# Expert stage of a one-core MoE decoder layer: f32r-split weight products against plain f32 products, experts taken in pairs

## The reference

```python
def hier_moe(h, w_group, b_group, w_expert, b_expert, w_gate, w_up, w_down):
    ...                                   # top-1 group of 4, top-2 of its 8 experts
    gates = jnp.sum(jax.nn.one_hot(e_idx, N_EXPERTS) * wts[..., None], axis=1)
    def expert(acc, prm):
        wg, wu, wd, gt = prm
        hid = jax.nn.silu(h @ wg) * (h @ wu)
        return acc + gt[:, None] * (hid @ wd), None
    out, _ = lax.scan(expert, jnp.zeros_like(h), (w_gate, w_up, w_down, gates.T))
```

## Time and profile before

| | us |
|---|---|
| median of 3 runs | 792.78 |
| lowest, highest | 792.27, 794.53 |
| profiled execution: span | 794.2 |
| TensorE (PE) busy | 728.8 |
| VectorE (DVE) busy | 636.6 |
| ScalarE (ACT) busy | 526.4 |
| GpSimd (POOL) busy | 307.2 |
| HBM read | 248.30 MB, 314 GB/s over the span |

### The profile page before, as it was taken

The page is one execution under the profiler, slowest core; times in us unless marked ns, Lnnn a source line. Parts: engine busy times, 40 slices in busy tenths (PEclk is TensorE's granted clock), DMA queues, the critical chain, the costliest instruction groups (busy, mean ns, idle before and its releaser), DMA issues.

```text
span 794.2 us, 12672 instructions
## 1 busy us (share of the span) xinstructions
PE 728.8 (92%) x4733; PEld 570.3 (72%) x4734; DVE 636.6 (80%) x538; ACT 526.4 (66%) x544; POOL 307.2 (39%) x214
## 2 busy tenths in 40 slices
PE   3669999989679999999999999999999999999980
PEld 1248577544457888888888888888888888888860
DVE  3363294635648999999999999999999999999973
ACT  2020133455527887888888888878888888888761
POOL 7300000040053456654456644566544566544000
PEclk9979999999659999999999999999999999999996
DMA  8999987710528899999999999999999999999501
GB/s 337 357 405 379 367 313 275 292 69 0 212 76 309 319 383 378 372 367 370 383 379 364 377 371 372 381 381 369 372 373 381 365 383 369 371 375 372 202 0 61
DMA packets 102004, 249.78 MB, mean 315 GB/s; under 512 B 8134, under 2 KB 8146, under 8 KB 98898
## 3 DMA queue, kind: packets, MB, share of 16 engines
q1 hardware_dynamic: 96448, 244.33, 82.9%
q10 hardware_dynamic: 5092, 3.46, 1.4%
q0 software_dynamic: 432, 1.59, 0.6%
HBM read 248.30 MB, written 1.07 MB: 314 GB/s over the span
## 4 chain that ended last, share of the span: by engine, by line
PE 84%; DVE 5%; DMA 4%; POOL 2%; ACT 2%; issue 2%; ACTq 0%; DVEq 0%; POOLq 0%
PE PS L1250 45%; PE PS L1238 8%; PE PS L1218 7%; PE PS L1209 6%; PE PS L1042 5%; PE PS L1160 3%; PE PS L1036 3%; POOL line L373 2%; DMA toe<-line_dram 2%; PE PS L1228 1%; DMA tabT<-in_rel_bias_dram 1%; PE PS L1017 1%; DVE MOD L698 1%; DVE S L774 1%; DVE S L754 1%
## 5 line engine op out<-in xcount | busy, mean ns | idle before, releaser
L918 DVE TENSOR_TENSOR WL<-W,WH 128x2048 fp32r<-128x2048 f32 x187 | 419.8, 2295 | 7.1 <-ACT WH L619 7.1
L619 ACT CAST WH<-W 128x2048 fp32r<-128x2048 f32 x187 | 349.9, 1903 | 48.6 <-PE PS L1250 48.6
L416 POOL TENSOR_SCALAR OG<-slot_no,cur 128x128 f32<-128x128 f32 x64 | 161.7, 2531 | 0.0
L1250 PE MATMUL PS<-WH,XT 128*128 128x512 f32 x512 | 140.2, 396 | 0.6 <-DVE XT L928 0.6
L1250 PE MATMUL PS<-WL,XT 128*128 128x512 f32 x508 | 140.0, 397 | 0.0
L403 POOL COPY cur<-PG 128x4 f32 (+1 forms) x33 | 8.3, 251 | 274.8 <-PE PS L1228 227.3
L1250 PEld LDWEIGHTS PS<-WH,XT 128*128 128x128 f32 x512 | 97.0, 190 | 23.8 <-DVE XT L928 0.6
L1250 PEld LDWEIGHTS PS<-WL,XT 128*128 128x128 f32 x508 | 96.0, 189 | 22.4
L413 POOL TENSOR_SCALAR OH<-slot_no,cur 128x128 bf16<-128x128 f32 x64 | 106.5, 1674 | 0.0
L1250 PE MATMUL PS<-WH,HT 128*128 128x512 f32 x256 | 70.5, 398 | 1.5 <-issue 1.5
L698 DVE SCALAR_TENSOR_TENSOR MOD<-W,cS,MOD 128x2048 f32<-128x2048 f32 x20 | 46.9, 2347 | 30.1 <-DMA W<-in_w_ada_dram 29.8
(11 more groups left out here) (184 smaller groups left out, 762.3 us busy)
## 6 DMA issues: line engine op xcount, KB each, us to landing
W<-in_w_gate_dram SPq DMA_DIRECT2D x64, 1024.0 KB, 8.0
W<-in_w_down_dram SPq DMA_DIRECT2D x64, 1024.0 KB, 6.2
W<-in_w_up_dram SPq DMA_DIRECT2D x63, 1024.0 KB, 9.9
W<-in_w_ada_dram SPq DMA_DIRECT2D x24, 1024.0 KB, 8.1
W<-in_w_in_dram SPq DMA_DIRECT2D x12, 1024.0 KB, 13.2
W<-in_w_out_dram SPq DMA_DIRECT2D x4, 1024.0 KB, 11.6
toe<-line_dram POOLq DMA_DIRECT2D x1, 1536.0 KB, 14.5
X<-in_x_dram ACTq DMA_DIRECT2D x1, 1024.0 KB, 12.4
```

What stands on the lines that cost most here:

```text
L416: nc.gpsimd.tensor_scalar(OG[:, buf, t, :], slot_no[:], cur[:, buf, 0, t:t + 1], cur[:, buf, 1, t:t + 1], ALU.is_equal, ALU.mult).then_inc ...
L619: nc.scalar.copy(WH[:, (UPE * odd + u) % SPLITS, :], source).then_inc(hi_ready, 1)
L918: nc.vector.tensor_tensor(low, source, WH[:, (UPE * odd + u) % SPLITS, :].bitcast(f32), ALU.subtract).then_inc(lo_ready, 1)
L1250: last = nc.tensor.matmul(PS[:, bank, :], lhsT, w[:, q * 512:(q + 1) * 512], start=begin, stop=end)
```

## The change

The expert stage is rewritten. The weights are no longer split: TensorE multiplies the f32 units as they arrive in W, with f32 token blocks and f32 hidden blocks as 64-column stationary operands. WH, WL, H3, GU, YH, YL, gcol, the SPARE unit and all expert work on GpSimd go; VectorE makes the one-hots. Two experts make a pair: they share one gather (f32, straight from Hn, 128 columns: 64 slots for each), one transpose of the gated one-hots and one scatter with 128 rows of YS. The even expert's products go to rows 0 to 63 of PSUM banks 0 and 1, the odd one's to rows 64 to 127. The hidden rows are made row-wise and transposed by `transpose_hidden`. The loop body holds two pairs; SP loads the units in the order in which TensorE uses them (`place_in_turn`). The first scatter starts the accumulation in place of four zeroing matmuls. Passes of 64 slots and the test of maxcnt stay.

The core of the diff, TensorE:

```diff
-            pe.wait_ge(h3_ready, TT)
             def one_pass(p):
-                def gather(n, buf, turn):
...
-                            for part in range(3):
-                                last = nc.tensor.matmul(PS[:, 2, k * SLOTS:(k + 1) * SLOTS], H3[:, part, t, k * P:(k + 1) * P],
-                                                        OH[:, buf, t, 0:SLOTS], start=(t == 0 and part == 0),
-                                                        stop=(t == TT - 1 and part == 2))
+                def gather(m, buf, part):
+                    pe.wait_ge(oh_ready, m + 1)
+                    if not isinstance(m, int) or m or part:
+                        pe.wait_ge(xt_ready, m * 2 + part)
+                    for k in range(4):
+                        for t in range(TT):
+                            last = nc.tensor.matmul(PS[:, 2, k * 2 * SLOTS:(k + 1) * 2 * SLOTS],
+                                                    Hn[:, t, (4 * part + k) * P:(4 * part + k + 1) * P],
+                                                    OH[:, buf, t].rearrange("p e s -> p (e s)"),
+                                                    start=(t == 0), stop=(t == TT - 1))
+                def slots_by_row(m, buf):
+                    pe.wait_ge(og_ready, m + 1)
+                    pe.wait_ge(ht_ready, m * 2 + 1)
+                    for t in range(TT):
+                        last = nc.tensor.transpose(PS[:, 3, c0:c0 + P], OG[:, buf, t].rearrange("p e s -> p (e s)"), ident[:])
+                def gate_up(i, odd, n, buf, used):
+                    rows = slice(SLOTS * odd, SLOTS * odd + SLOTS)
+                    pe.wait_ge(xt_ready, pairs_before(i, p) * 2 + 2)
+                    if used:
+                        pe.wait_ge(ys_ready, n - 1)
+                    for u in range(4):
+                        unit_arrived(pe, i, odd, u, p)
+                        w = W[unit_slot(i, odd, u)]
+                        for q in range(4):
+                            k = 4 * (u % 2) + q
+                            last = nc.tensor.matmul(PS[rows, u // 2, :], XT[:, buf, k, SLOTS * odd:SLOTS * odd + SLOTS],
+                                                    w[:, q * 512:(q + 1) * 512], start=(k == 0), stop=(k == DC - 1))
+                        last.then_inc(unit_used, 1)
+                def transpose_hidden(m, n, odd):
+                    pe.wait_ge(hid_ready, n + 1)
...
+                    for k in range(FC):
+                        last = nc.tensor.matmul(PS[:, 3, k * SLOTS:(k + 1) * SLOTS], HID[rows, k * P:(k + 1) * P],
+                                                ident[rows, rows], start=True, stop=True)
+                def down(i, odd, n):
+                    pe.wait_ge(ht_ready, n + 1)
+                    for u in (4, 5):
+                        unit_arrived(pe, i, odd, u, p)
+                        for q in range(4):
+                            k = 2 * (u - 4) + q // 2
+                            last = nc.tensor.matmul(PS[rows, q % 2, :], HT[:, k, :], w[:, q * 512:(q + 1) * 512],
+                                                    start=(k == 0), stop=(k == FC - 1))
+                def scatter(m, begin):
+                    pe.wait_ge(st_ready, m + 1)
+                    pe.wait_ge(ys_ready, m * 2 + 2)
+                    for t in range(TT):
+                        for half in range(2):
+                            last = nc.tensor.matmul(PS[:, 4 + 2 * t + half, :], ST[:, t * P:(t + 1) * P],
+                                                    YS[:, half * 512:half * 512 + 512],
+                                                    start=begin, stop=True, skip_group_check=True)
+                def pair(i, buf):
+                    gate_up(i, 0, n, buf, used)
+                    if not is_first(i):
+                        down(i - 1, 1, n - 1)
+                    transpose_hidden(m, n, 0)
+                    if not is_last(i):
+                        gather(m + 1, 1 - buf, 0)
+                    slots_by_row(m, buf)
+                    gate_up(i, 1, n + 1, buf, used)
+                    if not is_first(i):
+                        scatter(m - 1, is_one(i) and p == 0)
+                    down(i, 0, n)
+                    transpose_hidden(m, n + 1, 1)
+                    if not is_last(i):
+                        gather(m + 1, 1 - buf, 1)
+                gather(N_PAIRS * p, 0, 0)
+                gather(N_PAIRS * p, 0, 1)
+                by_pairs(pe, pair)
+                down(N_PAIRS - 1, 1, N_EXPERTS * (p + 1) - 1)
+                scatter(N_PAIRS * (p + 1) - 1, False)
```

ScalarE and VectorE:

```diff
+                def tokens(i, buf, part):
+                    act.wait_ge(gather_mm, m * 2 + (part + 1))
...
+                    nc.scalar.copy(XT[:, buf, 4 * part:4 * part + 4, :],
+                                   PS[:, 2, :].rearrange("p (k s) -> p k s", k=4)).then_inc(xt_ready, 1)
+                def silu(i, odd, n, used):
+                    wait_used(act, i, odd, 3, p)
+                    nc.scalar.activation(SG[rows, :], PS[rows, 0, :], ACT.Silu).then_inc(silu_ready, 1)
+                def output(i, odd, m, used):
+                    wait_used(act, i, odd, 5, p)
+                    nc.scalar.copy(YS[rows, :], PS[rows, 0:2, :].rearrange("p b f -> p (b f)")).then_inc(ys_ready, 1)
+                def pair(i, buf):
+                    silu(i, 0, n, used)
+                    if not is_first(i):
+                        output(i - 1, 1, m - 1, not is_one(i) or p > 0)
+                    if not is_last(i):
+                        tokens(i + 1, 1 - buf, 0)
+                    silu(i, 1, n + 1, used)
+                    output(i, 0, m, used)
+                    if not is_last(i):
+                        tokens(i + 1, 1 - buf, 1)
...
+                def onehot(i, buf, m):
+                    nc.vector.tensor_tensor(OH[:, buf], slots, column(0), ALU.is_equal).then_inc(oh_ready, 1)
+                    nc.vector.tensor_tensor(OG[:, buf], OH[:, buf], column(1), ALU.mult).then_inc(og_ready, 1)
+                def hidden(n, odd, used):
+                    dve.wait_ge(silu_ready, n + 1)
+                    nc.vector.tensor_tensor(HID[rows, :], SG[rows, :], PS[rows, 1, :], ALU.mult).then_inc(hid_ready, 1)
+                def hidden_columns(i, odd, n):
+                    dve.wait_ge(ht_mm, n + 1)
+                    nc.vector.tensor_copy(HT[:], PS[:, 3, 0:FC * SLOTS].rearrange("p (k s) -> p k s", k=FC)).then_inc(ht_ready, 1)
+                def slots(m):
+                    dve.wait_ge(st_mm, m + 1)
+                    nc.vector.tensor_copy(ST[:], PS[:, 3, FC * SLOTS:FC * SLOTS + SEQ]).then_inc(st_ready, 1)
+                def pair(i, buf):
+                    if not is_last(i):
+                        onehot(i + 1, 1 - buf, m + 1)
+                    hidden(n, 0, used)
+                    hidden_columns(i, 0, n)
+                    slots(m)
+                    hidden(n + 1, 1, used)
+                    hidden_columns(i, 1, n + 1)
```

More of the change, by code:

```diff
@@ new lines, in unit, with pair @@
+                def unit(i, odd, u):
+                    e = i * 2 + odd
+                    slot = unit_slot(i, odd, u)
+                    sp.dma_start(W[slot][:].rearrange("p (k f) -> p k f", k=unit_source(e, u).shape[1]),
+                                 unit_source(e, u)).then_inc(unit_in[slot], 16)
+                def pair(i, later):
+                    first = isinstance(i, int) and i == 0
+                    turn = [(i, 0, 0), (i, 0, 1), (i, 0, 2), (i, 0, 3)]
+                    if not first:
+                        turn += [(i - 1, 1, 4), (i - 1, 1, 5)]
+                    turn += [(i, 1, 0), (i, 1, 1), (i, 1, 2), (i, 1, 3), (i, 0, 4), (i, 0, 5)]
+                    for a, odd, u in turn:
+                        n = unit_number(a, odd, u, p)
+                        if later:
+                            sp.wait_ge(unit_used, n + (1 - RING))
+                        else:
+                            free(n)
+                        unit(a, odd, u)
@@ L941, in pair @@
[L941 to L956 removed]
+                    dve.wait_ge(pass_shift, p)
@@ L1232, in scatter @@
-                def scatter(n, buf):
-                    for y, ready in ((YH, yh_ready), (YL, yl_ready)):
-                        pe.wait_ge(ready, n + 1)
-                        for t in range(TT):
-                            for half in range(2):
-                                last = nc.tensor.matmul(PS[:, 4 + 2 * t + half, :], ST[:, buf, t * P:(t + 1) * P],
-                                                        y[:, half * 512:half * 512 + 512],
-                                                        start=False, stop=True, skip_group_check=True)
-                    last.then_inc(scat_mm, 1)
@@ L1243, in unit @@
-                def unit(n, at, spare, outs):
-                    for high in (True, False):
-                        pe.wait_ge(hi_ready if high else lo_ready, n + 1)
```

(15 more changed lines are left out.)

396 lines of the change are left out of this document (120 added, 276 removed).

## The result

Over four runs of each, the changed kernel takes 1062.83 us at the median (1057.76 to 1065.77) and the kernel before 793.53 (792.27 to 794.53). The ratio is 1.3391, 95% interval 1.3347 to 1.3436: 269 us slower. The forecast was 997 in a range of 984 to 1084. So the side and the range held, and the likeliest case was 66 us too low.

What follows compares the result with a forecast made beforehand. PE was taken to bound the expert stage, with DMA and DVE a few per cent behind. 232.6 before the loop + 747.5 for the loop + 18.0 behind it = 998 us, given as 997 against the median; range 984 to 1084.

Steps and rivals of the forecast that it cites:

- likeliest case: Whole kernel: gate_up and the other half's down run fully side by side, 46.3 us a pair, 997 us; chance 0.50.
- The start: Before the loop: maxcnt, one-hot and two gather halves with copies put the first weight matmul at about 232.6 us.
- the tail: From the last matmul to the end of the span: 18.0 us, taken from the kernel before.
- in-order rival: In each pair, down of the odd expert waits behind gate_up: 51.5 us a pair, 1075 us; chance 0.33.
- Price of an f32 matmul: Weight matmuls on PE: two records of 0.43 us each, 0.86 a matmul, 3.44 a unit against 1.85 today.
- full concurrency: Down of the odd expert runs beside the even expert's gate_up on the other column half: 6.9 us a pair vanish.
- the last 7 matmuls of gate_up: Shorter look-ahead at the gate_up to down border: 6.0 us a pair go, the sum hardly moves.
- wait (b): Before the even expert's transpose_hidden: PE waits for silu and the product, 1.7 us a pair unless down covers it.
- the 2 us for the clock: First gate matmuls of the loop run at a low clock: 2 us added once.
- Shallow look-ahead: Rival: two to four matmuls overlap per pair, 1.7 to 3.4 us, silu wait still covered; about 1035 us; chance 0.12.
- Wait (a): Next pair's first gate matmul waits for ACT's copy of XT's second half: 1.0 us a pair, bounds 0.8 to 1.2.
- the rivals in which the DMA binds: A 64-column matmul leaves one record, 0.43 us: PE 30.9 us a pair below DMA's 33.7, end at 769; chance 0.02.

Runs made afterwards that it cites:

- the gather between the halves: Changed kernel with the first half of the next pair's gather moved between the even expert's gate_up and the odd expert's down: 1094.76 us.
- the kernel with two borders: Changed kernel with the last four matmuls of the even expert's gate and up issued behind the eight of the odd expert's down: 1068.87 us.
- both experts abreast: Changed kernel with a pair's experts alternating matmul by matmul in gate, up and down, shared 128-row instructions, four full transposes: 744.69 us, 0.9389 of the kernel before.
- blocks of one: Changed kernel with the last eight gate and up matmuls of the even expert alternating one by one with the odd expert's eight down matmuls: 1016.84 us.

## Why the prediction was right, and where it was wrong

The loop, from the first weight matmul to the last scatter, was forecast at 747.5 us and took 1048.4 - 235.8 = 812.6, so 65.1 more. The start was 3.2 late and the tail 2.7 short. That is the whole of the 65.7 by which the span exceeds the forecast 998. The likeliest case alone, 984 to 1012, missed; the range held because it took in the in-order rival.

**Price of an f32 matmul: right.** Two records of 0.434 us at 64 columns. Its consequence was right too: 1.86 times the PE work a unit, PE alone binding, and the engines that were relieved giving nothing back.

**The step that failed**: "I take full concurrency because the second half's loads started at once, with nothing executed before them", and with it "If PE looks ahead only over the last 7 matmuls of gate_up the sum hardly moves". The row showed eight instructions of look-ahead, and eight was all there is: four records, in f32 two matmuls. In the row the first half *was* two matmuls, so it could show a start past them and nothing more. The text said so ("How much further than eight PE looks no row shows"), then took sixteen records for free, and the case it priced beside that, seven matmuls, left the sum where it was. Four records instead of sixteen: 5.2 us a pair come back, the wait (b) of 1.7 does not appear, and the small terms below add 1.0. So 4.46 a pair, 62.4 over the 14 middle pairs. The last pair, which loses the same overlap, and what follows it add 4.8 (1048.4 - 989.2 = 59.2, forecast 54.4), and the first pair gives some 2 back (43.1, forecast 44.9 with the 2 us for the clock).

**The rivals.** *In order* gave 1075 with 51.5 a pair; in turn it would have been 52.5 (the gather between the halves shows it). *Shallow look-ahead* named the mechanism: two to four matmuls, 1.7 to 3.4 us a pair, with (b) covered. The run lies at its lower end, 1.75. Its sum of 1035 was for the middle of that interval; its lower end would have come to 1075 - 14 x 1.7 = 1051, and the terms below (14 x 1.0) make up the rest. The Trainium skill's rule that MATMULs are "pc-monotone in start AND end" (page "TensorE: Matmul & The Clock Gate", section "What overlaps and what doesn't") would have given 52.5 a pair. The trace does not agree across column halves, where starts at 544.74 and 545.16 stand against program order, and agrees within a half and at full width.

**Terms that were a little off.** A record 0.434 and not 0.43: 0.4 a pair. The gather 2.05 + 1.89 = 3.9 and not 3.5: its records come every 0.118 us and not every 0.11, and PE passes from one kind of matmul to another at each end. The scatter 3.6 and not 3.4, the hidden transposes 2.06 and not 2.0. Wait (a) 0.85, forecast 1.0, bounds 0.8 and 1.2. Together 1.0 a pair. Wait (b) was covered by down, and is 1.57 where the cover goes (forecast 1.7). The rate of 373 GB/s, read as the DMA's own and level with PE, was what PE asked for: the loads reach 394. That touched only the rivals in which the DMA binds. And two executions differ by more than the 0.3% that the forecast allowed: the changed kernel's four spread over 0.8%.

**Start and tail.** The first weight matmul starts at 235.80, forecast 232.6. But 3.1 us of that are there before the change touches anything: maxcnt starts at 226.14, not at 223.01. In this execution PE waited 11.13 us for the load of toe at 48 us, against 7.63 in the profiled execution of before, and from there on it runs 3.1 behind. From the start of maxcnt to the first weight matmul it took 9.66 us, forecast 232.6 - 223.01 = 9.6. The 2 us for a low clock in the first gate matmuls were not needed: the granted clock reads 0.57 from 231 to 236 us and 1.00 from there to 252. It is low once more in the loop, 0.57 from 252 to 256 us, behind a wait (b) of 1.39 that nothing covers in the first pair; the gather there takes 3.60 us instead of 2.05. The tail is 15.3 us, forecast 18.0 as before. Some 2.0 of the 2.7 lie between the end of the last matmul and ACT's first square of the last norm, 4.6 us after and 6.6 before; why was not tried.

## What to carry to other kernels

A row that shows concurrency gives its depth as well: price only as much overlap as the row contains, and treat everything beyond as a separate case with its own sum. When work could run on two halves of PE's columns, write the program so that the halves alternate matmul by matmul; the same products and the same bytes took 1063 us in blocks and 745 alternated. A short idle of PE can cost more than its length where the granted clock falls behind it. And before an engine's work is traded for that of engines off the path, multiply out the price on the engine that binds.

## What the runs showed of the hardware

- PE starts a matmul on the other column half when four records of this half are left to run, the one that starts with it counted (544.74, beside 545.16 to 546.02), at each border anew (539.85 and 545.05 in the kernel with two borders), and also with no semaphore wait near the border. Four records are two f32 matmuls or four bf16 ones, eight instructions in both. A full-width gather between the halves ended it (32 records unbroken at 537.05). Whether PE counts records, instructions or moving columns (512 a record in both), and why four, no run here tells.
- Two 64-column matmuls side by side cost what one costs: 64 records in 13.95 us, and 32 one after the other take as long (f32, 512 moving columns).
- The DMA engines reach 394 GB/s with loads of 1 MB where enough of them are queued; the 373 of the earlier trace rows was read while PE was full. With both experts abreast the loads run at 394 throughout, while PE is busy 426 of the 460 us from 240 to 700 and never waits for one.
- An idle of some 1.5 us of PE can be followed by a stretch at a granted clock near 0.5: 0.59 from 480.2 to 483.6 us with blocks of one, where the gather took 3.39 us instead of 2.05.
